# Two-layer hybrid decoder trunk: TensorE takes the units of two attentions in pairs

## What is computed

```
x += 0.5 * post(FFN1(pre(x)));  x += post(MIX(pre(x)));  x += 0.5 * post(FFN2(pre(x)))
```

```
s = q . k * scale + bias (masked);  p = exp(s - max(s));  o = (p . v) / sum(p)
```

## Time and profile before

| | |
|---|---|
| median of 3 runs | 958.29 us (958.17 to 958.67) |
| the profiled execution | 958.22 us, span 956.5 us |
| granted TensorE clock | 0.999 of 2.4 GHz |
| busy, share of the span | PE 99%, DVE 80%, ACT 51%, POOL 12% |
| sliding attention | 219.8 to 231.3 us of the span |
| last attention | 713.6 to 746.2 us of the span |

### The profile page before, as it was taken

How to read it: one execution, slowest core, us unless ns; L and a number is a source line. 1 busy time by engine, 2 the same in 40 slices (tenths; PEclk the granted TensorE clock), 3 DMA queues, 4 the chain that set the end, 5 groups by cost and what they waited for, 6 DMA issues and landing times.

```text
span 956.5 us, 13887 instructions
## 1 busy us (share of the span) xinstructions
PE 949.5 (99%) x4900; PEld 793.5 (83%) x4900; DVE 764.5 (80%) x1464; ACT 489.7 (51%) x800; POOL 118.0 (12%) x128
## 2 busy tenths in 40 slices
PE   9999999999999999999999999999999999999997
PEld 8888888898888888888888888888788888888886
DVE  6889888759578888887888878877678588888884
ACT  7535343688464453445635353465567455443432
POOL 1200000155620000000200000012161420000000
PEclk9999999999999999999999999999999999999999
DMA  9875666242855657477084747516950436665621
GB/s 353 316 247 198 197 206 238 66 143 90 244 197 176 220 175 252 143 238 236 32 288 160 255 149 247 220 49 207 319 179 2 155 110 232 208 224 170 212 96 45
DMA packets 122293, 179.23 MB, mean 187 GB/s; under 512 B 3041, under 2 KB 97401, under 8 KB 121989
## 3 DMA queue, kind: packets, MB, share of 16 engines
q1 hardware_dynamic: 114740, 168.20, 52.4%
q10 hardware_dynamic: 7200, 9.31, 3.0%
q0 software_dynamic: 304, 1.09, 0.3%
HBM read 177.49 MB, written 1.09 MB: 187 GB/s over the span
## 4 chain that ended last, share of the span: by engine, by line
PE 98%; issue 1%; DMA 0%; DVE 0%; POOL 0%; ACT 0%; DVEq 0%; POOLq 0%
PE ps L1347 92%; PE ps L1630 2%; PE ps L1609 1%; PE ps L1388 1%; PE ps L1361 1%; PE ps L1809 0%; DMA lead<-in_first 0%; PE ps L1773 0%; PE ps L1473 0%; DVE x L1965 0%; DVEq L194 0%; POOLq L194 0%; POOL rstd L921 0%; DVE probt L2105 0%; PE ps L1822 0%
## 5 line engine op out<-in xcount | busy, mean ns | idle before, releaser
L1347 PE MATMUL ps<-w_hi,xt_hi 128*128 128x512 f32 (+4 forms) x914 | 351.8, 388 | 0.4 <-ACT w_hi L991 0.4
L1347 PE MATMUL ps<-w_hi,xt_lo 128*128 128x512 f32 (+3 forms) x912 | 348.9, 385 | 0.0
L1347 PE MATMUL ps<-w_lo,xt_hi 128*128 128x512 f32 (+3 forms) x912 | 348.4, 385 | 0.0
L1911 DVE TENSOR_TENSOR w_lo<-raw,w_hi 128x2048 fp32r<-128x2048 f32 (+3 forms) x103 | 225.6, 2228 | 44.6 <-ACT w_hi L954 44.1
L2011 DVE STREAM_TRANSPOSE ps<-h 32x128 f32<-32x128 f32 x624 | 201.4, 323 | 9.2
L1347 PEld LDWEIGHTS ps<-w_hi,xt_hi 128*128 128x128 f32 x914 | 171.7, 188 | 33.4 <-issue 1.1
L1347 PEld LDWEIGHTS ps<-w_hi,xt_lo 128*128 128x128 f32 x912 | 171.4, 188 | 33.3
L1347 PEld LDWEIGHTS ps<-w_lo,xt_hi 128*128 128x128 f32 x912 | 171.4, 188 | 32.5
L954 ACT ACTIVATE w_hi<-raw 128x2048 fp32r<-128x2048 f32 (+3 forms) x106 | 192.6, 1864 | 1.4 <-DMA raw<-in_l_ffn_wu 1.2
L1069 ACT ACTIVATE ht_hi<-ps 128x512 fp32r<-128x512 f32 x40 | 24.0, 599 | 285.6 <-DVE ps L2011 284.6
L1347 PE MATMUL ps<-down_hi,ht_hi 128*128 128x512 f32 x320 | 124.9, 390 | 0.0
(11 more groups left out here) (230 smaller groups left out, 790.4 us busy)
## 6 DMA issues: line engine op xcount, KB each, us to landing
raw<-in_l_ffn_wg SPq DMA_DIRECT2D x41, 1024.0 KB, 7.4
raw<-in_l_ffn_wu SPq DMA_DIRECT2D x41, 1024.0 KB, 9.8
raw_down<-in_l_ffn_wd SPq DMA_DIRECT2D x40, 1024.0 KB, 5.0
raw<-in_l_w_in SPq DMA_DIRECT2D x10, 1024.0 KB, 8.6
raw<-in_l_w_out SPq DMA_DIRECT2D x8, 1024.0 KB, 7.3
xn<-in_l_ffn_wd SPq DMA_DIRECT2D x4, 1024.0 KB, 7.3
raw<-in_l_w_in SPq DMA_DIRECT2D x4, 768.0 KB, 6.3
lead<-in_first SPq DMA_DIRECT2D x7, 384.0 KB, 6.4
```

The costliest lines, as they stand in the source:

```text
L1347: return pe.matmul(dst, lhs, rhs, start=start, stop=stop, skip_group_check=True)
L1911: dve.tensor_tensor(part(w_lo), part(raw), part(w_hi).bitcast(F32), ALU.subtract).then_inc(main_lo, 1)
```

## The change

In the sliding and the last attention PE goes by pairs of units; the latent attention keeps the old steps. For odd n a pair is: turn of n-5, values of n-7 and n-6, turn of n-4, scores of n-1 and n. The turning of the first rows of finished heads becomes a function of its own and stands in the last pair, in front of its values, that is behind values 36 and 37 of the last attention in place of in front of them. The lists of DVE and ACT are the same as before: there the lines only get a name (`turned_copy`, `behind = 2`). No DMA is moved.

```diff
@@ in the tensor engine's attention
                 def run():
+                    if by_pairs(base):
+                        for n in range(ahead // 2 * 2 + 1, count + LAG_V + 1, 2):
+                            pair(n)
+                        return
                     for n in range(ahead, count + LAG_V):
                         step(n)
+
+                def pair(n):
+
+                    turned_ahead = max(ahead - LAG_T, 0)
+                    if turned_ahead <= n - 5 < count:
+                        turn_probs(base + n - 5)
+                    if turned and n == count + LAG_V:
+                        turn_first_rows()
+                    for v in (n - 7, n - 6):
+                        if 0 <= v < count:
+                            values(base + v)
+                    if turned_ahead <= n - 4 < count:
+                        turn_probs(base + n - 4)
+                    for v in (n - 1, n):
+                        if ahead <= v < count:
+                            scores(base + v)
+                    for v in (n - 1, n):
+                        if v in aside:
+                            aside[v]()
...
                     if turned and n == count + LAG_T - 1:
-
-                        pe.wait_ge(logits_ready, units_by(base + count - 1))
-                        for v in range(base + count - (6 if base < LAST_BASE else 5), base + count - 3):
-                            pe.wait_ge(*copied(v))
-                        pe.wait_ge(head_out, OUT_AT[parts_of(base + count - 1)[0][0], 0])
-                        if turned == "out1":
-                            pe.wait_ge(branch_added, 4)
-                        turn_whole(attn, 0, turned)
+                        turn_first_rows()
```

More of the change, by code:

```diff
@@ L384, in turned_bank, with by_pairs @@
             return ps[:, own_bank(u), 0:SEQ]
+        def by_pairs(base):
+            return base != UNITS * ATT["mla"]
         def copied_by_act(u):
@@ L1161, in exps @@
                 ahead = AHEAD.get(name, 0)
-                for u in range(base + copies, base + ahead - 2):
+                behind = 2
+                for u in range(base + copies, base + ahead - behind):
                     if copied_by_act(u):
@@ L1170, in exps @@
                         aside[u - base]()
-                    if u - base >= 2 and copied_by_act(u - 2):
-                        copy(u - 2)
+                    if u - base >= 2 and copied_by_act(u - behind):
+                        copy(u - behind)
                     if u < UNITS and n % HEADS == HEADS - 1:
@@ L1645, in run, with turn_first_rows @@
                 def run():
+                    if by_pairs(base):
+                        for n in range(ahead // 2 * 2 + 1, count + LAG_V + 1, 2):
+                            pair(n)
+                        return
                     for n in range(ahead, count + LAG_V):
                         step(n)
+                def pair(n):
[15 more added lines that the diff above has]
+                            aside[v]()
+                def turn_first_rows():
+                    pe.wait_ge(logits_ready, units_by(base + count - 1))
+                    for v in range(base + count - (6 if base < LAST_BASE else 5), base + count - 3):
+                        pe.wait_ge(*copied(v))
+                    pe.wait_ge(head_out, OUT_AT[parts_of(base + count - 1)[0][0], 0])
+                    if turned == "out1":
+                        pe.wait_ge(branch_added, 4)
+                    turn_whole(attn, 0, turned)
                 def step(n):
@@ L2120, in run, with turned_copy @@
                         step(n)
+                def turned_copy(n):
+                    if LAG_T <= n < count + LAG_T and not copied_by_act(base + n - LAG_T):
+                        copy(base + n - LAG_T)
                 def step(n):
@@ L2126, in step @@
                         aside[n]()
-                    if LAG_T <= n < count + LAG_T and not copied_by_act(base + n - LAG_T):
-                        copy(base + n - LAG_T)
+                    turned_copy(n)
                     if n - LAG_T + 1 in sums:
```

## The result

The changed kernel takes 962.80 us (median of 6 runs, 962.39 to 964.05) against 958.23 us (6 runs, 958.14 to 958.67) for the kernel before: 1.0048 times as long, 95% interval 1.0035 to 1.0061. It is slower, in the direction of the forecast and by its mechanism, but by 4.6 us where 2.3 were forecast, and 0.4 us above the range. The profiled execution took 962.44 us with a span of 960.7 us, against 958.22 and 956.5 before: 4.2 us more. The granted clock is 0.999 before and 1.000 after, so no clock is in the difference.

The account below looks back on a forecast made before the run. PE, busy 99% of the span, was taken to bound the kernel; +1.5 us in the sliding attention and +0.8 in the last made +2.3 on 958.22, thus 960.5 us, range 956.6 to 962.4.

Parts of the forecast that it names:

- part 1: PE's new order: a turn instead of a score behind each value block gains 0.10 us, -1.7 last and -0.5 sliding attention.
- the waits: PE's odd values waiting for DVE copies: together 3.0 us in the last attention, 1.85 in the sliding one.
- a wait of odd values on DVE's copy: Copy of odd unit m stands behind logits of m+3 on DVE; values wait 0.19 us per 256-wide pair.
- the three links of the chain: First score to logits 0.53, logits to copy 0.34, copy to PE's values 0.47 us; PE unhindered arrives after 1.15.
- The row at 229.33: Turn behind values in the old sliding attention, 0.23 us against 0.22, taken as evidence for the 0.10 gain.
- The last attention in sum: Waits 3.0, gain -1.7, extra block +0.15, old waits of 0.34 and 0.32 gone: +0.8 us.
- The sliding attention, +1.5: Waits of odd values 1.85, gain -0.5, one more value block +0.15: +1.5 us.
- Win and moba pairs: Last attention's pairs taking win and moba by turns: a 0.08 us wait uses up the gain, period 1.46 again.
- No wait: Rival: copies come in time, only PE's order counts, -0.35 sliding and -2.2 last, 955.7 us; chance 0.13, including almost none.
- they cancel: Rival: DVE chain shorter by 0.05 to 0.10 over 25 waits, result 958.2 to 959.3 us; chance 0.22.
- The switch gives nothing: Rival: every successor of a value block pays 0.10, no 2.2 us gain, 962.7; chance 0.10, shared with DVE falling further behind.
- a gain of nothing: Lower bound for the 0.10 us gain per value block on PE, if whatever follows a block pays.

Follow-up runs that it names:

- e1: Changed kernel with DVE's copy of n-3 put in front of the logits of n in even steps of the two attentions; 959.00 us, 1.0006.
- e10: Changed kernel with a 128-column reduction on DVE in front of each of the 26 copies of odd units; 967.09 us, 1.0098.
- the old end: Changed kernel with even-step copies first on DVE and ACT, and PE's old steps behind the last scores; 957.40 us, 0.9989.
- e2: Changed kernel with both turns in front of the value products and the scores right behind these; 961.31 us, 1.0029.
- e12: Changed kernel with ACT copying odd units in place of even ones from each attention's ninth unit on; 962.23 us, 1.0043.

## Why the prediction fell short, point by point

The mechanism was right, and two terms of its sum were mis-sized: the gain of part 1, taken at 2.2 us, measured 1.1; and the waits, taken at 4.85 us, measured about 5.6. Together they are the 1.9 us between the forecast's +2.3 and the trace's +4.2.

- **Slower, by a wait of odd values on DVE's copy:** right, and shown. The place, the three links of the chain (1.34), the two pieces of the value block and the wait of 0.20 (forecast 0.19) are in the rows; e1 takes the wait away and 3.8 us with it, e10 deepens it. The listed waits on DVE are 11 in the last attention (forecast some 16) and 6 in the sliding one (forecast 7).
- **"Part 1 gains 0.10 for each block":** this step failed. A score no longer follows the block, but the turn that does takes 0.20 before the next score where it took 0.14, so 0.05 to 0.06 of the 0.10 stays. The row at 229.33, on which the 0.10 rested, has another turn behind it and not a score: it could not show this. Measured in unhindered pairs, 1.68 against 1.62 forecast. At 17 blocks and 0.05, the gain is 0.85 and not 1.7 in the last attention; at 5 blocks, 0.25 and not 0.5 in the sliding one.
- **The waits, "together 3.0 us" in the last attention:** too small by 0.6. I take the length of each value block, start to start, less the unhindered 0.61 (0.50 with win and moba units):

| values | 3 | 5 to 11 | 13 | 15 | 17, 21, 23, 25 | 29, 31 | 33, 35 | 37 |
|---|---|---|---|---|---|---|---|---|
| forecast | 0.27 | 0.76 | 0.38 | 0.21 | 0.32 | 0.12 | 0.38 | 0.49 |
| measured | 0.32 | 1.00 | 0.32 | 0.29 | 0.29 | 0.11 | 0.51 | 0.40 |

The pattern is the forecast's, the sums 2.93 and 3.24. In the measured row is a cost that no row of before shows: a block that was held up ends dearer, 0.39 from its second half to the turn (722.70 to 723.09) where an unhindered half takes 0.33. Over the 13 blocks held up by 0.1 or more that is an estimated 0.7 us, more than the excess of 0.3, so without it the waits would have been a little shorter than forecast. The other 0.4 us of waits (forecast 0.07) are scores: three of them, at 735.41, 736.97 and 741.50, last 0.12 to 0.14 longer than their like. One of them, timeline, with the only row that ends at that moment:

```profile
735.34 0.36 ACT L1149 ACTIVATE probt<-ps 128x256 f32<-128x256 f32 x1
...
735.41 0.48 PE L1352 MATMUL ps<-mix_k,end_hi 128*128 128x256 f32 x2
...
735.76 0.33 PE L1352 MATMUL ps<-moba_k,down_lo 128*128 128x128 f32 x1
```

The second score begins 0.06 after ACT's copy ends. The profile names no releaser there; that it is this copy is read from the times and from e1, where the same kind of wait is named.
- **The last attention in sum:** ahead of score 39 the forecast was +0.3 and the trace has +1.75; 0.85 of the difference is the gain, 0.6 the waits. Behind score 39, forecast +0.5 (0.19 + 0.49 + 0.15 - 0.32), measured +0.54.
- **The sliding attention, +1.5:** its seven blocks are held up by 0.12, 0.25, 0.40, 0.28, 0.30, 0.30 and 0.35, 2.0 us against 1.85. With the 0.25 of the gain that did not come this gives +1.9, as measured.
- **Win and moba pairs:** forecast 1.46, measured between 1.41 (738.53 to 739.94) and 1.57 (730.87 to 732.44), 1.52 on average over the seven from 730.87 to 741.50. Unhindered they take 1.41, where 1.38 was in the sum.
- **The rivals.** *No wait* and *they cancel* didn't come. *The switch gives nothing* would have been 962.7, within 0.1 of what was measured, but that is a coincidence: pairs do get cheaper, by half of the term in dispute (1.1 us), and the waits are some 0.8 us longer than forecast, which nearly makes up for it. The Trainium skill (page TensorE: Matmul & The Clock Gate, section Architectural detail: the array is 16× 32×32, not 1× 128×128) says that PE's queue can pull weight loads ahead of matmuls in flight. What the prediction drew from it, that a switch of kinds would be hidden, is not borne out here: 20 gaps of 0.17 us stand in front of value products, and the order of neighbours changes a pair by 0.05.
- **What would have made the range right:** to ask of the turn behind a value block what stands behind that, and to take the bound "a gain of nothing" (named, but used for one rival only) half into the likeliest case.

Open: the causes inside PE of the 0.06 behind a turn and of the dearer end of a held-up block are not known; the runs show only where they are. Of the last attention's 1.5 us above the forecast, the gain (0.85) and the waits (0.6) leave less than 0.1.

## What to carry to other kernels

When one engine's order of issue is changed, follow each result once around the loop through the in-order lists of all engines: here PE's new order was worth 0.05 us a pair, and the usual 256-wide pair waited 0.24 until DVE's and ACT's lists were changed with it (962.8, 959.0 and 958.2 us). Only with the old end as well was it a gain, of 0.1%, just clear of noise. Moving one step or giving it to another engine (e2, e12) moved the wait and did not remove it. To price a switch between kinds of instruction, take whole periods of a pair that did not wait, since the cost of a block can turn up two instructions behind it.

## What the runs showed of the hardware

- A score that follows a turn of 256 columns (two transposes) starts 0.14 us after it (717.86 to 718.00 before), and 0.19 to 0.20 after it where value products stood in front of the turn (717.24 to 717.44 and 723.09 to 723.28 after).
- Value products held up in the middle of a block cost 0.05 to 0.06 us more to the next instruction than the wait itself (0.39 against 0.33 from their second half to it).
- On DVE a memset of 6 columns (0.06 us) ran beside the copy issued behind it and cost nothing that the time shows (962.64 us against 962.80); a reduction of 128 columns is busy for 0.28 us and delays what is behind it by 0.20.
